# Norm behind each projection: the squares of tiles 0 to 5 summed by VectorE in PSUM, TensorE multiplies the sum and two tiles at the end

## The chip, the core and the metric

One core of a Trainium2 chip runs the whole program. The metric is the device time of one execution in microseconds (us), as the median of several runs.

## What is computed

Two transformer blocks over 256 positions and 1024 channels, one after the other, in float32. Most of the work is large matrix products; between them stand root-mean-square norms over the channels:

```python
def rms_norm(x, g):
    xf = x.astype(jnp.float32)
    y = xf * lax.rsqrt(jnp.mean(xf * xf, axis=-1, keepdims=True) + NORM_EPS)
    return (y * g.astype(jnp.float32)).astype(x.dtype)

# first block
    mix = jnp.concatenate([o_rw, o_nsa, o_s5], axis=-1).astype(h.dtype) @ w_out[i]
    h = h + rms_norm(mix, post_mix_norm[i])                              # norm 1
    f = conv_ffn(rms_norm(h, pre_ffn_norm[i]), w_up[i], conv_w[i], conv_b[i], w_down[i])   # norm 2
    h = h + rms_norm(f, post_ffn_norm[i])                                # norm 3
    e = rms_norm(p[i] @ w_ple[i], ple_norm[i])                           # norm 4
    gate = jax.nn.sigmoid((h @ w_ple_gate[i]).astype(jnp.float32)).astype(h.dtype)
    h = h + gate * e
# second block, for each of two layers
        h = _modulate(_rmsnorm(x, norm1_g[layer]), sh1, sc1)             # norms 5 and 7
        ...
        x = x + g1[:, None, :] * y
        h = _modulate(_rmsnorm(x, norm2_g[layer]), sh2, sc2)             # norms 6 and 8
        x = x + g2[:, None, :] * _conv_ffn(h, ffn_w_up[layer], ...)
    return _rmsnorm(x, final_g)                                          # norm 9
```

## The kernel before

**Tiles.** The residual `h` lies transposed: 8 tiles of 128 channels by 256 positions. A projection has 8 output tiles (`job`s), each in one of the 8 PSUM banks, which are handed out in rotation (`next_bank`, line 477); TensorE waits until the bank's last job has been read by the engine that frees it (`freed`). `close` (535) counts `psum_ready` up by one when a job is done, and readers wait for their job's number.

**Split weights.** Products of a projection are made in three passes (`three_passes`, 558): high part of the weight by high part of the activation, high by low, low by high. A weight chunk is 128 by 2048 floats (two output tiles). SyncE's queue loads it into one of 6 ring slots. ScalarE writes its high part (`hi_ready`), GpSimd subtracts and writes the low part (`low_parts`, 1531, `lo_ready`), strictly in the order in which the chunks are used; there are 4 slots for high parts. `chunk` (509) makes TensorE wait for `lo_ready` of a chunk the first time that it is asked for.

**When ScalarE makes high parts.** It has no fixed place for them. Every time that ScalarE is about to wait for a job (`take` 2327, `gone` 2331), `reach` (2303) first emits all the high parts that are due: those whose chunk four places back in the order (its high slot) and six places back (its ring slot) are used only by jobs before that one. `take0` and plain waits emit none. `root` (2357) and `high_parts` (2361, the high parts of the normalised activations) use these plain waits.

**A norm.** ScalarE squares the tiles (`squares` 2347 for norms 6 to 9, two tiles per instruction for tiles 0 to 5, once VectorE has added the job to `h`; `out_squares` 2567 for norms 1 and 3, from PSUM and together with a copy). TensorE sums over the channels: for every tile two matmuls with the squares as the stationary operand and one column of 1/1024 (`mean_square_of` 603). Then ScalarE takes the root (`root`), VectorE the reciprocal (`norm_scale` 1613), TensorE spreads it over the partitions (`spread` 614), VectorE scales, ScalarE writes the high parts, and TensorE starts the next projection with `first_tiles` (584). This function first opens four tiles and asks for their weights, two chunks, and only then waits for the high part of activation tile 0; it runs the high passes of the four tiles together, k by k, and then the low passes.

**Where the squares are multiplied.** In `last_tile` (634; norms 1, 6, 8) tiles 0 to 5 stand ahead of the last output tile and 6 and 7 behind it. In TensorE's `ffn` (1101; norms 3, 7, 9), whose down projection goes over m = 0 to 3 with two output tiles and three chunks (`("down", f, m, c)`) each, tiles 0 to 3 stand ahead of chunk c = 1 of m = 3, tiles 4 and 5 ahead of c = 2, and 6 and 7 behind.

The chunks behind the down projection of ffn 0 are `("pleg", 0 to 3)`, read by the jobs `pg`; behind that of ffn 1 stand `("kv", 0)`, `("kv", 4)`, `("kv", 8)`, `("kv", 12)`, read by `dk` and `dv`. After norm 3 ScalarE comes to its next `reach` at `take(("pg", 0))` (2635), after norm 7 at `reach(("dk", 0, 0, 0))` (2676).

Of the kernel before, what the change touches and what calls it, by code (L numbers as in the profile page):

```python
# [73 lines left out]
def two_block_kernel(nc, a, out):  # L74
    ctx = ExitStack()
    with ctx:
# [306 lines left out]
        NORM_ORDER = (0, 1, 2, 4, 3, 5, 6, 7, 8, 9)  # L383

        def rs_of(i):
            return rs[:, 4:8] if i == 4 else rs[:, 0:4]
# [69 lines left out]
        def _(pe):  # L456
# [34 lines left out]
            def held_back():  # L491
# [3 lines left out]
                return bank  # L495

            begun = set()

# [84 lines left out]

            def first_tiles(rnd, jobs, x, ks=tuple(range(KT))):

                low, high = x
                todo = []
                for job, key, c0 in jobs:
                    b = opened(job)[:, 0:T]
                    todo.append((b, [v[:, :, c0:c0 + P] for v in chunk(key)]))  # L590
                for n, k in enumerate(ks):
                    pe.wait_ge(sem("x_high"), KT * (rnd + 1) + n + 1)
                    for b, (w_lo, w_hi) in todo:
                        mm(b, w_hi[:, k, :], high[:, k, :], start=(n == 0), stop=False)
                        mm(b, w_lo[:, k, :], high[:, k, :], start=False, stop=False)
                for t, (b, (_, w_hi)) in enumerate(todo):
# [4 lines left out]
                    close(last)  # L601

            def mean_square_of(i, b, sq, ks):

                for k in ks:
                    if k % 2 == 0 or k == KT - 1:
                        pe.wait_ge(sem("squares"), 5 * (i - (i > 4)) + (1, 1, 2, 2, 3, 3, 4, 5)[k])
                    for s in range(2):
                        last = mm(b[:, s:s + 1], sq[:, k, s * P:s * P + P], ones_mean[:, 0:1],
                                  start=(k == s == 0), stop=(k == KT - 1), skip_group_check=True)  # L610
                if ks[-1] == KT - 1:
                    close(last)

            def spread(i, scratch=True):
# [8 lines left out]
            def projection(rnd, name, key, x, ms=None, ks=tuple(range(KT))):  # L623

                tiles = [((name, m), (key, m // 2), 128 * (m % 2)) for m in range(8)]
                first_tiles(rnd, tiles[:4], x, ks)
# [474 lines left out]
            def ffn(f, first, ms):  # L1101
# [5 lines left out]
                for m in range(4):  # L1107
# [14 lines left out]
                    for c in range(3):  # L1122
                        if m == 3 and c:
                            mean_square_of(ms[0], b_ms, ms[1], (0, 1, 2, 3) if c == 1 else (4, 5))
                        key = ("down", f, m, c)
                        w = chunk(key)
                        n = chunk_src[key][0].shape[1]
                        for i in range(2):
                            for k in range(n):
                                t = 8 * c + k  # L1130
                                if m == 0 and i == 0:
                                    pe.wait_ge(sem("act_split"), FT * f + t + 1)
                                last = three_passes(outs[i][:, 0:T], [v[:, k, i * P:i * P + P] for v in w],
                                                    (act_lo[:, t, :], act_hi[:, t, :]), t == 0, t == FT - 1)
                            if c == 2:
                                close(last)
                        if c < 2:
# [192 lines left out]
            pe.wait_ge(sem("x_high"), KT * 10)  # L1330
            pe.wait_ge(sem("x_split"), KT * 10)
            for m, bank in enumerate(out_banks):
                numbered(("dw", m), bank)
                held.remove(bank)
                close(out_passes(m, bank, (6, 7)))
            split_tile(("dw", 6), ("do", 3), 0, (hn_lo, hn_hi))
# [210 lines left out]
        def _(dve):  # L1547
# [62 lines left out]
            def own_done(n):  # L1610
                dve.wait_ge(sem("dve_own"), n)

            def norm_scale(i):
# [468 lines left out]
            def ffn(f):  # L2082
# [47 lines left out]
                if f:  # L2130
                    for m in range(8):
                        b = take(("down", f, m))
                        stt(h[:, m, :], b[:, 0:T], mc(f - 1, 5, m), h[:, m, :], MUL, ADD, *freed(("down", f, m)))

            def modulated(i, n, rnd, low, high, shift, **k):

                return scaled_parts(i, lambda k: gsc[:, 8 * n + k:8 * n + k + 1], rnd, high, low, sem("x_scaled"), shift, **k)

            add_normed(1, "post_mix", yb)
            scaled_parts(2, lambda k: col("pre_ffn", k), 1, hn_hi, hn_lo, sem("x_scaled"))  # L2140
# [24 lines left out]
            for k in range(KT):  # L2165
                stt(eb[:, k, :], eb[:, k, :], col("ple_norm", k), wide, MUL, MUL, sem("eb_scaled"))
            add_normed_split(3, "post_ffn", yb, 2, hn_hi, hn_lo)
            dve.wait_ge(sem("h_copied"), KT)
# [32 lines left out]
            for m in range(8):  # L2201
                b = take(("po", m))
                stt(h[:, m, :], b[:, 0:T], mc(0, 2, m), h[:, m, :], MUL, ADD, *freed(("po", m)))
            settle()
            modulated(6, 1, 5, hn_lo, hn_hi, 24)
# [63 lines left out]
            for m in range(8):  # L2269
                b = take(("dw", m))  # L2270
                stt(h[:, m, :], b[:, 0:T], mc(1, 2, m), h[:, m, :], MUL, ADD, *freed(("dw", m)))
            settle()
            modulated(8, 4, 9, hn_lo, hn_hi, 72)
# [10 lines left out]
        def _(act_):  # L2284
# [45 lines left out]

            def gone(job):

                reach(job)
                act_.wait_ge(*freed(job))
# [277 lines left out]

            out_squares([("out", m) for m in range(8)], yb)
            root(1)
# [8 lines left out]
            for k in range(0, KT, 2):  # L2623
                af(hn[:, k:k + 2, :], eb[:, k:k + 2, :], ACT.Square, sem("eb_squares"))
            out_squares([("down", 0, m) for m in range(4)], yb)
            root(4)
            out_squares([("down", 0, m) for m in range(4, 8)], yb, 4)
            root(3)
# [38 lines left out]
            for m in (6, 7):  # L2667
                pooled(m)
            squares(hn, lambda k: gone(("po", k)))
# [75 lines left out]
            attention_high((6, 7))  # L2745
            squares(hn2, lambda k: gone(("dw", k)))
            root(8)
            modulate(8, 6, hn_hi, 72)
            ffn(2)
            squares(hn, lambda k: gone(("down", 2, k)))  # L2750
            root(9)
# [31 lines left out]
```

## Time and profile before

| | |
|---|---|
| median of 3 runs | 1455.54 us (1453.73 to 1458.12) |
| the profiled execution | 1459.26 us, its span 1457.3 us |
| mean granted TensorE clock | 0.949 of full |
| TensorE matmul busy | 1362.4 us, 93% |
| GpSimd / ScalarE / VectorE busy | 833.8 / 619.2 / 562.4 us |

The profile comes from one execution. Its timeline gives start and duration of each instruction (equal neighbours are merged, with their count), and in brackets how long the engine sat idle before it and who released it. The chain of work that ended last is followed back from the last instruction.

### The profile page before, as it was taken

What the parts mean: (1) busy time and instruction counts of PE and PEld (TensorE: products, weight loads), DVE (VectorE), ACT (ScalarE), POOL (GpSimd) and SP (SyncE); (2) the same over time, 40 slices, a digit from 0 to 9 for tenths busy, and PEclk for the clock granted to TensorE, in tenths of its full rate; (3) what the DMA queues carried; (4) which work ended last, traced back from release to release, by engine and by line L of the source; (5) the groups of instructions that cost most, each with busy time, mean ns of one, the idle gap of its engine ahead of it and who ended that gap; (6) DMA issues with size and microseconds to landing.
All of it is one profiled execution on the core that took longest, in us unless ns stands there. A gap on an engine that the chain in (4) does not pass through costs nothing.

```text
span 1457.3 us, 26522 instructions
## 1 busy us (share of the span) xinstructions
PE 1362.4 (93%) x11138; PEld 1277.3 (88%) x11138; DVE 562.4 (39%) x1241; ACT 619.2 (42%) x925; POOL 833.8 (57%) x419
## 2 busy tenths in 40 slices
PE   6989798979899999989999999999999987999998
PEld 5987355868899999989999999989999877999997
DVE  4645867651255472322433302132233242333301
ACT  3532153223465554544444434544544343554431
POOL 5872430022388878545688775845655443688771
PEclk9998798996899999989999999999999999899998
DMA  7945898330455555434455554443636683455550
GB/s 219 207 123 188 301 383 312 120 112 4 134 171 185 175 180 179 140 108 149 141 177 193 166 188 146 140 132 91 186 91 216 192 286 102 158 178 192 167 159 30
DMA packets 246323, 244.96 MB, mean 168 GB/s; under 512 B 25652, under 2 KB 215230, under 8 KB 246206
## 3 DMA queue, kind: packets, MB, share of 16 engines
q1 hardware_dynamic: 245715, 243.10, 52.2%
q8 instruction: 89, 1.46, 0.4%
q10 hardware_dynamic: 491, 0.17, 0.1%
q14 instruction: 28, 0.23, 0.1%
HBM read 242.20 MB, written 1.05 MB: 167 GB/s over the span
## 4 chain that ended last, share of the span: by engine, by line
PE 83%; DVE 6%; issue 2%; ACT 2%; DMA 2%; POOL 0%; DVEq 0%; ACTq 0%
PE banks L533 82%; DVE arena L1584 2%; DMA ring<-in_attn_w_o_dram 1%; DVE arena L1591 1%; ACT arena L2291 1%; DMA ring<-in_ffn_w_up_dram 1%; PE banks L543 0%; DVE banks L1591 0%; ACT ring_hi L2291 0%; DVE ring_lo L1584 0%; DVE arena L1772 0%; PE banks L818 0%; DVE arena L1588 0%; DVE hn L1591 0%; PE banks L941 0%
## 5 line engine op out<-in xcount | busy, mean ns | idle before, releaser
L1535 POOL TENSOR_TENSOR ring_lo<-ring,ring_hi 128x2048 fp32r<-128x2048 f32 (+1 forms) x176 | 718.7, 4096 | 510.4 <-ACT ring_hi L2291 510.0
L533 PE MATMUL banks<-hn_hi,ring_lo 128*128 128x256 f32 x1888 | 539.1, 289 | 0.0
L533 PE MATMUL banks<-hn_hi,ring_hi 128*128 128x256 f32 x1696 | 484.4, 290 | 7.6 <-ACT hn_hi L2291 7.6
L533 PE MATMUL banks<-hn_lo,ring_hi 128*128 128x256 f32 x1696 | 445.0, 283 | 0.0
L2291 ACT ACTIVATE ring_hi<-ring 128x2048 fp32r<-128x2048 f32 (+1 forms) x176 | 299.7, 1704 | 179.7 <-PE banks L533 131.0
L533 PEld LDWEIGHTS banks<-hn_hi,ring_lo 128*128 128x128 f32 x1888 | 375.2, 199 | 0.0
L533 PEld LDWEIGHTS banks<-hn_hi,ring_hi 128*128 128x128 f32 x1696 | 335.0, 198 | 9.6 <-issue 9.4
L533 PEld LDWEIGHTS banks<-hn_lo,ring_hi 128*128 128x128 f32 x1696 | 310.9, 193 | 0.1
L2291 ACT ACTIVATE arena<-banks 128x256 f32<-128x256 f32 (+5 forms) x229 | 90.3, 411 | 319.1 <-PE banks L533 265.4
L533 PEld LDWEIGHTS banks<-arena 64*128 64x128 f32 (+4 forms) x1282 | 122.7, 188 | 72.4 <-issue 52.3
L533 PE MATMUL banks<-arena 128*64 128x128 f32 (+9 forms) x1282 | 150.4, 314 | 32.1 <-issue 13.2
L533 PE MATMUL banks<-act_hi,ring_hi 128*128 128x256 f32 x528 | 150.1, 284 | 0.0
L533 PE MATMUL banks<-act_hi,ring_lo 128*128 128x256 f32 x528 | 149.4, 283 | 0.0
L533 PE MATMUL banks<-act_lo,ring_hi 128*128 128x256 f32 x528 | 149.4, 283 | 0.0
L1591 DVE SCALAR_TENSOR_TENSOR arena<-banks,par,arena 128x255 f32<-128x255 f32 (+1 forms) x187 | 89.1, 480 | 151.6 <-ACT arena L2291 149.9
L2291 ACT ACTIVATE arena<-banks,par 128x256 f32<-128x256 f32 x88 | 49.8, 565 | 121.5 <-PE banks L533 121.4
L533 PEld LDWEIGHTS banks<-act_lo,ring_hi 128*128 128x128 f32 x528 | 101.3, 192 | 0.0
L533 PEld LDWEIGHTS banks<-act_hi,ring_hi 128*128 128x128 f32 x528 | 101.3, 192 | 0.0
L533 PEld LDWEIGHTS banks<-act_hi,ring_lo 128*128 128x128 f32 x528 | 101.3, 192 | 0.0
L1591 DVE SCALAR_TENSOR_TENSOR h<-banks,mod,h 128x256 f32<-128x256 f32 x32 | 15.5, 484 | 163.4 <-PE banks L533 163.4
L533 PE MATMUL banks<-hn_hi,early_hi 128*128 128x256 f32 x192 | 58.6, 305 | 7.6 <-DVE ring_lo L1584 6.4
L533 PE MATMUL banks<-ring_lo,hn_hi 128*128 128x256 f32 (+1 forms) x224 | 63.7, 284 | 0.0
(236 smaller groups left out, 1706.0 us busy)
## 6 DMA issues: line engine op xcount, KB each, us to landing
ring<-in_ada_w_dram SPq DMA_DIRECT2D x48, 1024.0 KB, 8.3
ring<-in_ffn_w_up_dram SPq DMA_DIRECT2D x44, 1024.0 KB, 5.2
ring<-in_w_up_dram SPq DMA_DIRECT2D x22, 1024.0 KB, 5.1
ring<-in_ffn_w_down_dram SPq DMA_DIRECT2D x16, 1024.0 KB, 5.4
ring<-in_w_kv_dram SPq DMA_DIRECT2D x15, 1024.0 KB, 5.4
ring<-in_w_kv_dram SPq DMA_DIRECT2D x18, 512.0 KB, 3.9
ring<-in_attn_w_q_dram SPq DMA_DIRECT2D x18, 512.0 KB, 3.9
ring<-in_w_in_dram SPq DMA_DIRECT2D x8, 1024.0 KB, 12.1
```

The source lines that it names most:

```text
L533: return nc.tensor.matmul(o, l, r, start=start, stop=stop, **k)
L1535: led.emit(g.tensor_tensor(low, raw, high.bitcast(F32), ALU.subtract), sem("lo_ready"))
L1584: led.emit(v.tensor_tensor(o, x, y, op), signal, value)
L1591: led.emit(v.scalar_tensor_tensor(out=o, in0=x, scalar=s, in1=y, op0=op0, op1=op1), signal, value)
L2291: led.emit(nc.scalar.activation(o, x, func, **k), signal, value)
```

## The change

Norms 1, 3, 6, 7, 8 and 9 are `SUMMED`. For these ScalarE writes the square of tile 0 into a PSUM bank of its own, the job `("acc", i)`, which is opened ahead of the projection's first tile and held until the norm's last matmul. VectorE adds the squares of tiles 1 to 4 to it in place and writes the sum with tile 5 to the place of the square 0 in SBUF. TensorE multiplies no squares ahead of the last tile; behind it it multiplies the sum, tile 6 and tile 7. ScalarE's squares are now one instruction for each tile, and for the output tiles 6 and 7 it calls no `reach` (`limit` 0, or `take0` in place of `take`).

```diff
             def first_tiles(...): ...
+                if ms is not None:
+                    gathered(ms)
...
             def mean_square_of(i, b, sq, ks):
                 for k in ks:
-                    if k % 2 == 0 or k == KT - 1:
-                        pe.wait_ge(sem("squares"), 5 * (i - (i > 4)) + (1, 1, 2, 2, 3, 3, 4, 5)[k])
+                    if i in SUMMED and k == 0:
+                        copied(("acc", i))
+                    elif i in SUMMED:
+                        pe.wait_ge(sem("squares"), square_base[i] + k + 1)
+                    elif k % 2 == 0 or k == KT - 1:
+                        pe.wait_ge(sem("squares"), square_base[i] + (1, 1, 2, 2, 3, 3, 4, 5)[k])
...
             def last_tile(job, key, x, ms):
                 b = opened(job)
                 b_ms = opened(("ms", ms[0]))
-                mean_square_of(ms[0], b_ms, ms[1], (0, 1, 2, 3, 4, 5))
                 ...
-                mean_square_of(ms[0], b_ms, ms[1], (6, 7))
+                mean_square_of(ms[0], b_ms, ms[1], (0, 6, 7))
...
             def ffn(f, first, ms):
+                    if m == 0:
+                        gathered(ms[0])
...
-                        if m == 3 and c:
-                            mean_square_of(ms[0], b_ms, ms[1], (0, 1, 2, 3) if c == 1 else (4, 5))
...
-                mean_square_of(ms[0], b_ms, ms[1], (6, 7))
+                mean_square_of(ms[0], b_ms, ms[1], (0, 6, 7))
...
+            def add_square(i, k, sq):                     # VectorE
+                acc = bank_of(("acc", i))[:, 0:T]
+                dve.wait_ge(sem("squares"), square_base[i] + k + 1)
+                if k == 1:
+                    take(("acc", i))
+                else:
+                    own_done(summed_at[i, k - 1])
+                if k < 5:
+                    tt(acc, sq[:, k, :], acc, ADD)
+                    summed_at[i, k] = led.count["dve_own"]
+                else:
+                    tt(sq[:, 0, :], sq[:, k, :], acc, ADD, *freed(("acc", i)))
...
             for m in range(8):                            # VectorE, norm 8; 6, 7 and 9 alike
                 b = take(("dw", m))
                 stt(h[:, m, :], b[:, 0:T], mc(1, 2, m), h[:, m, :], MUL, ADD, *freed(("dw", m)))
+                if 2 <= m <= 6:
+                    add_square(8, m - 1, hn2)
...
-            def gone(job):
-                reach(job)
+            def gone(job, limit=99):
+                reach(job, limit)
                 act_.wait_ge(*freed(job))
...
+            def summed_squares(i, dst_, after):           # ScalarE
+                sqrt_table()
+                for k in range(KT):
+                    after(k)
+                    o = dst_[:, k, :] if k else take0(("acc", i))[:, 0:T]
+                    af(o, h[:, k, :], ACT.Square, sem("squares"))
...
-            def out_squares(jobs, y, k0=0):
+            def out_squares(i, jobs, y, k0=0):
                 sqrt_table()
                 for k, job in enumerate(jobs, k0):
-                    b = take(job)
-                    af(sqb[:, k, :], b[:, 0:T], ACT.Square, sem("squares") if k % 2 or k == 6 else None)
+                    b = take(job) if k < 6 else take0(job)
+                    o = sqb[:, k, :] if k else take0(("acc", i))[:, 0:T]
+                    af(o, b[:, 0:T], ACT.Square, sem("squares"))
                     af(y[:, k, :], b[:, 0:T], ACT.Identity, *freed(job))
...
-            squares(hn, lambda k: gone(("down", 1, k)))
+            summed_squares(7, hn, lambda k: gone(("down", 1, k), 99 if k < 6 else 0))
```

## Rows read from the trace of the kernel before

**Rows 1.** The page's part 4: shares of the chain that ended last, by engine.
```profile
PE 83%; DVE 6%; issue 2%; ACT 2%; DMA 2%; POOL 0%; DVEq 0%; ACTq 0%
```
**Rows 2.** Timeline, TensorE, norms 1 and 7: matmuls of squares (start us, duration us).
```profile
372.87 2.74 PE L533 MATMUL banks<-ones_mean,arena 128*128 128x1 f32 x24
...
885.47 1.84 PE L533 MATMUL banks<-ones_mean,hn 128*128 128x1 f32 x16
...
893.01 0.95 PE L533 MATMUL banks<-ones_mean,hn 128*128 128x1 f32 x8
...
899.40 0.60 PE L533 MATMUL banks<-ones_mean,hn 128*128 128x1 f32 x4 [0.68 <-ACT hn L2291]
```
**Rows 3.** Timeline, ScalarE, around norm 7.
```profile
880.49 0.63 ACT L2291 ACTIVATE hn<-h 128x512 f32<-128x512 f32 x1 [3.41 <-DVE h L1591]
881.02 1.90 ACT L2291 ACTIVATE ring_hi<-ring 128x2048 fp32r<-128x2048 f32 x1
...
893.21 1.92 ACT L2291 ACTIVATE ring_hi<-ring 128x2048 fp32r<-128x2048 f32 x1 [5.63 <-PE banks L533]
896.77 0.42 ACT L2291 ACTIVATE hn<-h 128x256 f32<-128x256 f32 x1 [1.65 <-DVE h L1591]
...
907.33 0.48 ACT L2291 ACTIVATE hn_hi<-banks,mod 128x256 fp32r<-128x256 f32 x1 [0.44 <-DVE banks L1591]
907.71 1.91 ACT L2291 ACTIVATE ring_hi<-ring 128x2048 fp32r<-128x2048 f32 x1
```
**Rows 4.** Timeline, GpSimd, around norm 7.
```profile
883.00 9.28 POOL L1535 TENSOR_TENSOR ring_lo<-ring,ring_hi 128x2048 fp32r<-128x2048 f32 x2 [2.34 <-ACT ring_hi L2291]
...
909.69 4.64 POOL L1535 TENSOR_TENSOR ring_lo<-ring,ring_hi 128x2048 fp32r<-128x2048 f32 x1 [9.89 <-ACT ring_hi L2291]
```
**Rows 5.** Timeline, TensorE: first matmul after norm 7; first of the fifth tile.
```profile
902.61 0.36 PE L533 MATMUL banks<-hn_hi,ring_hi 128*128 128x256 f32 x1 [1.18 <-ACT hn_hi L2291]
...
915.68 0.28 PE L533 MATMUL banks<-hn_hi,ring_hi 128*128 128x256 f32 x1
```
**Rows 6.** Timeline, ScalarE, around norm 3.
```profile
574.58 1.92 ACT L2291 ACTIVATE ring_hi<-ring 128x2048 fp32r<-128x2048 f32 x1
...
587.77 1.92 ACT L2291 ACTIVATE ring_hi<-ring 128x2048 fp32r<-128x2048 f32 x1 [5.63 <-PE banks L533]
...
604.57 1.91 ACT L2291 ACTIVATE ring_hi<-ring 128x2048 fp32r<-128x2048 f32 x1
```
**Rows 7.** Timeline, TensorE: first matmul after norm 3; first of the fifth tile.
```profile
597.16 0.55 PE L533 MATMUL banks<-hn_hi,ring_hi 128*128 128x256 f32 x1 [1.81 <-ACT hn_hi L2291]
...
611.13 0.28 PE L533 MATMUL banks<-hn_hi,ring_hi 128*128 128x256 f32 x1
```
**Rows 8.** Stretch after norm 6: PE, PEld, DVE, ACT, POOL busy; granted clock, DMA, GB/s.
```profile
703.00:708.00 5.00, 4.97 (x23) 5.00 (x24) 4.82 (x12) 2.81 (x7) 0.00 (x0) 0.50 0.05 12
```
**Rows 9.** Timeline, ScalarE and TensorE, around norm 8.
```profile
1236.05 1.91 ACT L2291 ACTIVATE ring_hi<-ring 128x2048 fp32r<-128x2048 f32 x1 [1.64 <-DMA ring<-in_ffn_w_up_dram]
...
1238.54 1.87 PE L533 MATMUL banks<-ones_mean,arena 128*128 128x1 f32 x8 [3.02 <-ACT arena L2291]
1240.26 0.56 PE L533 MATMUL banks<-hn_hi,ring_hi 128*128 128x256 f32 x1
...
1245.01 0.50 PE L533 MATMUL banks<-ones_mean,arena 128*128 128x1 f32 x4
...
1246.84 0.26 ACT L2291 ACTIVATE rs<-banks,drv 128x2 f32<-128x2 f32 x1 [0.69 <-PE banks L533]
```
**Rows 10.** The page's part 5: busy us, mean ns of one; idle before, and its releaser.
```profile
L1591 DVE SCALAR_TENSOR_TENSOR h<-banks,mod,h 128x256 f32<-128x256 f32 x32 | 15.5, 484 | 163.4 <-PE banks L533 163.4
```
**Rows 11.** Timeline, TensorE and GpSimd, after norm 2.
```profile
399.09 0.35 PE L533 MATMUL banks<-hn_hi,ring_hi 128*128 128x256 f32 x1 [1.09 <-ACT hn_hi L2291]
...
405.87 4.63 POOL L1535 TENSOR_TENSOR ring_lo<-ring,ring_hi 128x2048 fp32r<-128x2048 f32 x1 [26.96 <-ACT ring_hi L2291]
...
410.68 0.28 PE L533 MATMUL banks<-hn_hi,ring_hi 128*128 128x256 f32 x1
```

More of the change, by code:

```diff
@@ L383, in two_block_kernel @@
         NORM_ORDER = (0, 1, 2, 4, 3, 5, 6, 7, 8, 9)
+        SUMMED = (1, 3, 6, 7, 8, 9)
+        square_base, square_count = {}, 0
+        for i in NORM_ORDER:
+            square_base[i] = square_count
+            square_count += 8 if i in SUMMED else 0 if i == 4 else 5
         def rs_of(i):
@@ L495, in held_back, with gathered @@
                 return bank
+            def gathered(i):
+                numbered(("acc", i), held_back())
             begun = set()
@@ L582, in split_rows, with first_tiles @@
                 close(last)
-            def first_tiles(rnd, jobs, x, ks=tuple(range(KT))):
+            def first_tiles(rnd, jobs, x, ks=tuple(range(KT)), ms=None):
                 low, high = x
                 todo = []
+                if ms is not None:
+                    gathered(ms)
                 for job, key, c0 in jobs:
@@ L600, in first_tiles @@
                         last = mm(b, w_hi[:, k, :], low[:, k, :], start=False, stop=(n == KT - 1))
-                    close(last)
+                    close(last, 2 if ms is not None and t == 0 else 1)
             def mean_square_of(i, b, sq, ks):
                 for k in ks:
-                    if k % 2 == 0 or k == KT - 1:
-                        pe.wait_ge(sem("squares"), 5 * (i - (i > 4)) + (1, 1, 2, 2, 3, 3, 4, 5)[k])
+                    if i in SUMMED and k == 0:
[4 more added lines that the diff above has]
+                        pe.wait_ge(sem("squares"), square_base[i] + (1, 1, 2, 2, 3, 3, 4, 5)[k])
                     for s in range(2):
@@ L612, in mean_square_of @@
                     close(last)
+                    if i in SUMMED:
+                        held.remove(bank_no["acc", i])
             def spread(i, scratch=True):
@@ L625, in projection @@
                 tiles = [((name, m), (key, m // 2), 128 * (m % 2)) for m in range(8)]
-                first_tiles(rnd, tiles[:4], x, ks)
+                first_tiles(rnd, tiles[:4], x, ks, ms[0] if ms else None)
                 for t in tiles[4:7]:
@@ L1135, in ffn @@
                             if c == 2:
-                                close(last)
+                                close(last, 2 if m == i == 0 else 1)
                         if c < 2:
@@ L1331, in _ @@
             pe.wait_ge(sem("x_split"), KT * 10)
+            gathered(8)
             for m, bank in enumerate(out_banks):
@@ L1334, in _ @@
                 held.remove(bank)
-                close(out_passes(m, bank, (6, 7)))
+                close(out_passes(m, bank, (6, 7)), 1 if m else 2)
             split_tile(("dw", 6), ("do", 3), 0, (hn_lo, hn_hi))
@@ L1611, in own_done @@
                 dve.wait_ge(sem("dve_own"), n)
+            summed_at = {}
+            def add_square(i, k, sq):
[10 more added lines that the diff above has]
+                    tt(sq[:, 0, :], sq[:, k, :], acc, ADD, *freed(("acc", i)))
             def norm_scale(i):
@@ L2133, in ffn @@
                         stt(h[:, m, :], b[:, 0:T], mc(f - 1, 5, m), h[:, m, :], MUL, ADD, *freed(("down", f, m)))
+                        if 2 <= m <= 6:
+                            add_square(7 if f == 1 else 9, m - 1, hn)
             def modulated(i, n, rnd, low, high, shift, **k):
                 return scaled_parts(i, lambda k: gsc[:, 8 * n + k:8 * n + k + 1], rnd, high, low, sem("x_scaled"), shift, **k)
+            for k in range(1, 6):
+                add_square(1, k, sqb)
             add_normed(1, "post_mix", yb)
@@ L2166, in _ @@
                 stt(eb[:, k, :], eb[:, k, :], col("ple_norm", k), wide, MUL, MUL, sem("eb_scaled"))
+            for k in range(1, 6):
+                add_square(3, k, sqb)
             add_normed_split(3, "post_ffn", yb, 2, hn_hi, hn_lo)
@@ L2203, in _ @@
                 stt(h[:, m, :], b[:, 0:T], mc(0, 2, m), h[:, m, :], MUL, ADD, *freed(("po", m)))
+                if 2 <= m <= 6:
+                    add_square(6, m - 1, hn)
             settle()
@@ L2271, in _ @@
                 stt(h[:, m, :], b[:, 0:T], mc(1, 2, m), h[:, m, :], MUL, ADD, *freed(("dw", m)))
+                if 2 <= m <= 6:
+                    add_square(8, m - 1, hn2)
             settle()
@@ L2611, in ffn @@
                         own(1, j + 1)
-            out_squares([("out", m) for m in range(8)], yb)
+            out_squares(1, [("out", m) for m in range(8)], yb)
             root(1)
@@ L2624, in _ @@
                 af(hn[:, k:k + 2, :], eb[:, k:k + 2, :], ACT.Square, sem("eb_squares"))
-            out_squares([("down", 0, m) for m in range(4)], yb)
+            out_squares(3, [("down", 0, m) for m in range(4)], yb)
             root(4)
-            out_squares([("down", 0, m) for m in range(4, 8)], yb, 4)
+            out_squares(3, [("down", 0, m) for m in range(4, 8)], yb, 4)
             root(3)
@@ L2668, in _ @@
                 pooled(m)
-            squares(hn, lambda k: gone(("po", k)))
+            summed_squares(6, hn, lambda k: gone(("po", k), 99 if k < 6 else 0))
             root(6)
@@ L2745, in _ @@
             attention_high((6, 7))
-            squares(hn2, lambda k: gone(("dw", k)))
+            summed_squares(8, hn2, lambda k: gone(("dw", k), 99 if k < 6 else 0))
             root(8)
@@ L2749, in _ @@
             ffn(2)
-            squares(hn, lambda k: gone(("down", 2, k)))
+            summed_squares(9, hn, lambda k: gone(("down", 2, k), 99 if k < 6 else 0))
             root(9)
```

## The prediction

> **What bounds the kernel now.** I read the chain of work that ended last first: 83% of it is TensorE [rows 1]. So a matmul that is taken out of TensorE's stream is worth its full time, and every wait of TensorE costs its full time. Then I read the timeline around each norm, engine by engine. TensorE's rows show what is taken out [rows 2]. ScalarE's show which instructions stand between its squares [rows 3, 6], and this is the part that decides. GpSimd's show how long a low part takes [rows 4], and TensorE's again when the next projection starts and when its first four tiles are done [rows 5, 7, 11].
>
> The profiled execution took 1459.26 us, 3.7 above the median of 1455.54; I make the sum against the profiled one and take the difference to the median.
>
> **What it removes.** Per norm, 12 matmuls ahead of the last tile (two for each of the tiles 0 to 5). Norm 1 shows them as 24 records in 2.74 us, norm 7 as 1.84 + 0.95 = 2.79 us; the last record's drain is in these, so I take 2.7. TensorE stands in full work on either side, so all of it comes off: 6 x 2.7 = 16.2 us.
>
> The Trainium skill (TensorE: Matmul & The Clock Gate, Back-to-back issue gap) would make them cheaper: matmuls of one column follow each other at about 25 ns. By that the 24 records would be worth 0.6 us and all six norms 3.6 us. The rows show 114 ns a record [rows 2], and the measurement decides.
>
> **What it adds on TensorE.** Two matmuls with the sum at the very end, 2.79 / 12 x 2 = 0.46 us. In norms 6, 7 and 9 they lie in the wait for square 7: tile 6's four records (about 0.5 us) are followed by 0.68 us of idleness [rows 2], so they cost nothing; were the wait gone, they would cost 0.46. In norms 1 and 3 ScalarE squares straight from PSUM, VectorE's step of 0.48 us [rows 10] isn't in that wait, and I let them cost 0.3 each: -0.6 us of gain.
>
> **What it adds elsewhere.** ScalarE gets eight short squares for five; a single one took 0.42 us and a double one 0.63 [rows 3], and it has gaps of 1.7 to 5.6 us there. VectorE gets five adds. No add of this kind is in the rows; the nearest step on a tile takes 0.48 us [rows 10], so 2.4 us a norm, spread over a projection of over 20 us: nothing, or 0.5 where an add stands ahead of the last tile's step. The held bank leaves seven for the rotation; only norm 8 comes near it (below). SyncE's queue waits for the use of chunks by TensorE alone and is moved past nothing.
>
> **What it moves: ScalarE's high parts.** This is where I expect the loss. `gone` and `take` for output tiles 6 and 7 emit no high parts any more. Which stood there? In norm 7, between the square of tiles 4 and 5 (880.49) and that of tile 6 (896.77), ScalarE made three high parts, the first at 881.02, the last at 893.21 [rows 3]. By the rule of `reach` these are kv0, kv4 and kv8: their high slots are last used by the jobs 5 and 6, and so they become due at `gone(6)`, not before. Now they are skipped. `root` and `high_parts` don't emit any, so the next occasion is `reach(("dk", 0, 0, 0))`, behind the eighth high part of the activations, which ends at 907.33 + 0.48 = 907.81 in the times of before. There one high part was made (907.71, kv12); now there are four, kv0 first. And `first_tiles` asks for kv0 and kv4 before it multiplies anything.
>
> - kv0 high: 907.71 + 1.91 = 909.62. GpSimd starts at 909.69, as it did with kv12 [rows 4], and takes 4.64: 914.33. kv4's low part follows, 4.64 (9.28 for two): about 919.0.
> - TensorE starts at 919.0 in place of 902.61 [rows 5], 16.4 us later.
> - Its four first tiles took 13.07 us to 915.68. With all inputs there, the 96 matmuls take 11.59 us, as after norm 2 [rows 11], and in addition what the clock costs: 1.5 to 2.4 us, the excess of the blocks after norms 7 and 3 over it [rows 5, 7]. So they end at 919.0 + 13.4 = 932.4, 16.7 us later than before.
>
> Norm 3 is the same with pleg0, pleg1, pleg2: three high parts from 574.58 to 587.77, and the next `reach` at 604.57 [rows 6]. pleg0 high ends at 606.48, its low part at 611.2, pleg1's at 615.85; the start moves from 597.16 to 615.85. The four tiles took 13.97 us, to 611.13 [rows 7]; now they end at 615.85 + 13.4 = 629.25, 18.1 us later. Together 34.8 us. Later chunks don't add: kv8's low part is ready at 923.6, and needed at 932.
>
> Does something later give it back? Only a wait for a DMA could, if the DMA ran on by itself. But each DMA waits for a slot that TensorE frees, so the stream moves with TensorE. I take no return.
>
> **The clock.** After norm 6 the granted clock is 0.50 for 5 us [rows 8], the lower of its two levels, behind a few us in which TensorE had little to do. A longer idle stretch starts at the same level, so I charge the 1.5 to 2.4 us once per start, as before.
>
> **Norms 1, 6, 8: one high part late, but in time.** Here two of the chunks behind were due earlier, and only ug1 is skipped. It takes uu1's place at the `reach` behind the activations. After norm 2 that low part ran from 405.87 to 410.50, and TensorE comes to ug1 at 410.68 [rows 11]: 0.2 us of room, more after norms 6 and 8, where the first four tiles run at the low clock. Bounds 0 to 1 us each; I take 0.
>
> **Norm 8.** Before, TensorE waited ahead of the last tile for squares 4 and 5, because ScalarE stood at a high part whose weights had not landed (1236.05); it went on at 1238.54, and the last tile ran from 1240.26 to 1245.01, at the low clock [rows 9]. The change takes the wait from that place. What is late next? The last tile and the norm take the banks of dw4 and dw5. VectorE frees them behind its adds of squares 2 and 3; ScalarE was done with these squares at 1236.05 - 1.64 = 1234.4, and four steps of at most 0.48 [rows 10] take VectorE to about 1236.3, when TensorE starts the last tile. It ends at 1239.2 (24 x 0.12, the pitch of rows 11) or, if the clock has fallen, at 1241.1 (4.75 us, as before). VectorE's last step is queued behind the add of square 4, the step of dw6 and the add of square 5: ScalarE gives square 4 at about 1238.4, so this is at 1239.8. From the later of the two: 0.48, 0.42 and two matmuls of 0.60: the root starts at 1241.3 to 1242.9 in place of 1246.84, 3.9 to 5.5 us earlier. I take 4.6, with the 2.7 in it.
>
> **Sum.** Gains: norms 1 and 3: 2.4 each, norms 6, 7, 9: 2.7 each, norm 8: 4.6: 17.5 us. Losses: 34.8 us. Net +17.3: 1476.6 against 1459.26, as a median 1455.54 + 17.3 = 1472.8 us, slower by 1.2%.
>
> **Rivals.**
> - *Faster: the weights aren't in the way.* If TensorE could start after norms 3 and 7 without the skipped high parts, only the gains are left: 1455.5 - 17.5 = 1438.0 us. For it: 16.2 us of matmuls go for certain. Against it: the three high parts stand in the trace exactly where the change skips them, and the read of `lo_ready` is ahead of the first matmul. Chance 0.08.
> - *No change: only one of the two starts is late,* or each by half: 34.8 / 2 = 17.4 against 17.5, 1455.4 us. This needs a `reach` that I have overlooked. Chance 0.05.
> - *Slower still: the squeezed order costs more.* The 0.2 us of room after norm 2 goes, norms 6 and 8 get a stall of their own, and norm 8 gains nothing but its 2.7: 3 x 1 + 1.9 + some 2 for cold starts: 1480 us. It decides where GpSimd's low part of ug1 ends behind the fourth tile. Chance 0.12.
> - The forecast, both starts late by 16 to 19 us each: chance 0.75.
>
> **How the numbers follow.** Bounds of the likeliest case: losses 16.2 to 17.5 (norm 7) and 17.5 to 19 (norm 3), gains 15 to 19.5: net +14 to +21.5 (16.2 + 17.5 - 19.5; 17.5 + 19 - 15), and 2 us for the median: 1468 to 1478. With the third rival the range is 1465 to 1480; the two rivals below it hold 0.13. What can be told from no change is 0.3%, 4.4 us. Slower by more: 0.75 + 0.12 = 0.87. Within: 0.05. Faster: 0.08.
>
> **What would show it.** Right: after norms 3 and 7 TensorE idle for some 19 to 21 us, released by GpSimd's low parts; ScalarE with four high parts in a row behind the activations; no high parts between tiles 5 and 7; no squares ahead of the last tile; TensorE's matmul records fewer by 6 x 20 = 120. Wrong: TensorE starting a few us after the root in norms 3 and 7. The sum would then be off by the whole 34.8 us; nothing else in it is larger than 3 us.

## The result and the profile after

The changed kernel takes 1471.97 us (median of 4 runs, 1468.58 to 1474.35) against 1454.63 us (median of 4) for the kernel before in the same session: a ratio of 1.0125, 95% interval 1.0098 to 1.0152. It is slower by 17.3 us. The forecast said +17.3 and 1472.8 us.

The page's part 1 (busy us, share of the span, instructions), first of the kernel before, then of the changed one:

```profile
PE 1362.4 (93%) x11138; PEld 1277.3 (88%) x11138; DVE 562.4 (39%) x1241; ACT 619.2 (42%) x925; POOL 833.8 (57%) x419
PE 1335.0 (91%) x11018; PEld 1250.2 (85%) x11018; DVE 570.0 (39%) x1271; ACT 621.3 (42%) x937; POOL 833.2 (57%) x419
```

TensorE has 120 records fewer than the 11138 of before, so the matmuls are gone, and the kernel is slower all the same. The waits of TensorE, grouped by what ended them (us in total, times, longest), say where the time went. The two longest waits, 20.5 and 17.6 us, are new; the longest of before was 6.8 us.

```profile
PE banks L543 <- ACT hn_hi L2335: 23.4, 6, 17.6
PE banks L543 <- POOL ring_lo L1553: 20.5, 1, 20.5
```

They are the starts behind norms 3 and 7. First norm 3, its timeline on three engines (start us, duration us, engine, line, operation; in brackets the idle time before it and its releaser). ScalarE (root, then four high parts of weights), GpSimd (their low parts), TensorE (first matmul, which [rows 7] shows for before):

```profile
577.64 0.26 ACT L2335 ACTIVATE rs<-banks,drv 128x2 f32<-128x2 f32 x1 [0.58 <-PE banks L543]
...
588.15 7.31 ACT L2335 ACTIVATE ring_hi<-ring 128x2048 fp32r<-128x2048 f32 x4
```
```profile
590.14 18.05 POOL L1553 TENSOR_TENSOR ring_lo<-ring,ring_hi 128x2048 fp32r<-128x2048 f32 x4 [29.26 <-ACT ring_hi L2335]
```
```profile
599.47 0.55 PE L543 MATMUL banks<-hn_hi,ring_hi 128*128 128x256 f32 x1 [20.54 <-POOL ring_lo L1553]
```

The four high parts stand in one row behind the activations' eight, where [rows 6] has one. GpSimd had been idle for 29.26 us and then makes four low parts at 4.5 us each. TensorE starts when the second of them is done (590.14 + 9.0 = 599.2). Behind norm 7 it is the same. Here is ScalarE from the square of tile 5 to the weights' high parts; [rows 3] is its counterpart:

```profile
880.08 0.42 ACT L2335 ACTIVATE hn<-h 128x256 f32<-128x256 f32 x1 [1.74 <-DVE h L1609]
893.75 0.42 ACT L2335 ACTIVATE hn<-h 128x256 f32<-128x256 f32 x1 [13.26 <-DVE h L1609]
...
897.03 0.26 ACT L2335 ACTIVATE rs<-banks,drv 128x2 f32<-128x2 f32 x1 [0.70 <-PE banks L543]
...
904.31 0.47 ACT L2335 ACTIVATE hn_hi<-banks,mod 128x256 fp32r<-128x256 f32 x1 [0.43 <-DVE banks L1609]
904.69 7.30 ACT L2335 ACTIVATE ring_hi<-ring 128x2048 fp32r<-128x2048 f32 x4
```

The reader is to see the idle 13.26 us ahead of the square at 893.75: that is where the three high parts of [rows 3] stood. ScalarE now sits still there and has the work later, where TensorE waits for it. GpSimd and TensorE in the same place:

```profile
906.66 18.10 POOL L1553 TENSOR_TENSOR ring_lo<-ring,ring_hi 128x2048 fp32r<-128x2048 f32 x4 [26.34 <-ACT ring_hi L2335]
```
```profile
916.01 0.55 PE L543 MATMUL banks<-hn_hi,ring_hi 128*128 128x256 f32 x1 [17.60 <-ACT hn_hi L2335]
```

The profile puts this last wait down to ScalarE's `hn_hi`, but that had been written at 904.31 + 0.47. The wait covers several semaphores, and the second low part, done at about 915.7 (906.66 + 2 x 4.5), is what came last.

The start behind the root (first matmul minus root) is the measure for everything below: norm 3 from 3.10 to 21.83 us, norm 7 from 2.57 to 18.98 us.

### The profile page after: what moved, and what is told of

Same layout as the page of the kernel before. It is cut to its first block and busy times, and to the rows that moved or that the text cites. A ratio compares the mean times of both kernels' runs of the same rounds, so it can differ in the third digit from the quotient of the medians.

```text
span 1466.7 us, 26353 instructions
## 1 busy us (share of the span) xinstructions
PE 1335.0 (91%) x11018; PEld 1250.2 (85%) x11018; DVE 570.0 (39%) x1271; ACT 621.3 (42%) x937; POOL 833.2 (57%) x419
```

## Experiments

Three measures are used. The ratio and its interval come from the timed runs. The two starts behind the root come from the trace. So does the time from the root of norm 1 to the root of norm 9 (the start of ScalarE's rows `rs<-banks,drv`); it leaves out the stretch ahead of root 1, which takes 367 to 382 us in the traces (last section). It is no fine measure either: between root 1 and root 7 two_early_5 and norm8_order have the same instructions, and their traces differ by 4.4 us there (509.97 against 514.33). So a difference of a few us in this column says nothing by itself. "Start 3" and "start 7" are the first matmul behind the root of norm 3 and of norm 7; they hardly vary.

```
kernel                          median us  ratio   95% interval    start 3  start 7  root 1 to 9
before                          1454.6     -       -                3.10     2.57    1066.8
changed                         1472.0     1.0125  1.0098-1.0152   21.83    18.98    1088.5
early_37    3 high parts back   1435.4     0.9851  0.9820-0.9883    3.27     2.56    1051.7
early_all   no limit anywhere   1436.6     0.9865  0.9834-0.9896    3.10     2.57    1052.7
early_3     norm 3 alone back   1456.2     1.0013  0.9990-1.0036    3.10    18.99    1069.3
old_late_37 before + limit      1491.4     1.0232  1.0204-1.0260   21.82    19.00    1102.0
one_early   1 high part back    1462.4     1.0055  1.0035-1.0075   17.37    14.52    1077.4
two_early   2 high parts back   1431.6     0.9830  0.9764-0.9897    3.10     2.57    1051.2
at_root     3 behind the root   1457.1     0.9999  0.9976-1.0022   11.51    11.48    1070.5
squares_out matmuls dropped     1437.7     0.9874  0.9825-0.9922    3.10     2.57    1050.5
two_early_5 as two_early        1437.2     0.9882  0.9856-0.9909    3.10     2.56    1050.3
norm8_order ug0, uu0 moved      1436.7     0.9885  0.9858-0.9912    3.21     2.57    1054.8
```

**The theory** was the forecast's: the high parts that tiles 6 and 7 no longer make cost the two starts, and the rest of the change gains 17.5 us. **The rivals**: the time is lost in the other parts (adds, held bank, late multiplication); the loss is partly given back later; the loss is ScalarE's own time and not GpSimd's.

### Putting the high parts back

```diff
-                    b = take(job) if k < 6 else take0(job)
+                    b = take(job) if k < 6 or i == 3 else take0(job)
...
-            summed_squares(7, hn, lambda k: gone(("down", 1, k), 99 if k < 6 else 0))
+            summed_squares(7, hn, lambda k: gone(("down", 1, k)))
```

> The changed kernel, with the weights' high parts of norms 3 and 7 back where they stood (tile 6 of these two stages makes them again); everything else of the change stays, norms 1, 6, 8 and 9 keep the limit. Theory (deferred high parts): both starts are early again, and only the gains are left: 1455 - 17.5 = 1437 us (1433 to 1442), TensorE starting 2.6 us after root 7 and about 3 us after root 3. Rival A (the adds, the held bank or the late multiplication cost the time, and the high parts only lie beside it): it stays at 1465 to 1472. Rival B (part of the loss had come back later in the stream, so that undoing it gives less): 1443 to 1455.

Measured 1435.4 us, 0.9851 of before: two lines turn a kernel slower by 17 us into one faster by 20. From root 1 to root 9 it is 36.8 us shorter than the changed kernel; the two starts alone make 18.56 + 16.42 = 35.0 of this. ScalarE ahead of the root of norm 7 in this kernel:

```profile
862.17 1.90 ACT L2335 ACTIVATE ring_hi<-ring 128x2048 fp32r<-128x2048 f32 x1
867.08 1.92 ACT L2335 ACTIVATE ring_hi<-ring 128x2048 fp32r<-128x2048 f32 x1 [3.02 <-PE banks L543]
872.84 1.91 ACT L2335 ACTIVATE ring_hi<-ring 128x2048 fp32r<-128x2048 f32 x1 [3.84 <-PE banks L543]
875.52 0.42 ACT L2335 ACTIVATE hn<-h 128x256 f32<-128x256 f32 x1 [0.76 <-DVE h L1609]
...
878.80 0.26 ACT L2335 ACTIVATE rs<-banks,drv 128x2 f32<-128x2 f32 x1 [0.70 <-PE banks L543]
```

The three are back in the gap, and none delays a square: that of tile 6 still waits 0.76 us for VectorE. TensorE then starts 2.56 us behind the root:

```profile
881.36 0.55 PE L543 MATMUL banks<-hn_hi,ring_hi 128*128 128x256 f32 x1 [1.18 <-ACT hn_hi L2335]
```

In norm 7 no high part was in the way of the squares; start 3 is 3.27 us behind its root, so norm 3 doesn't suffer either.

### No limit in any norm

The same for norms 1, 6, 8 and 9 (`take(job)` and `gone(...)` without a limit everywhere).

> The changed kernel with no limit anywhere: norms 1 and 6 to 9 too make their high parts at tile 6. Theory: in norms 1, 6 and 8 ug1 was late but in time, so this is within 2 us of the kernel that restores norms 3 and 7 alone, 1437 us. If norms 1, 6 and 8 had a stall of their own from the limit (0.2 us of room), it is up to 3 us faster than that one. If instead the high part ahead of squares 6 and 7 lengthens the norm, it is 1 to 4 us slower.

Measured 1436.6 us, 1.2 above early_37 with overlapping intervals, and 1.0 us more between roots 1 and 9. In these norms the limit neither costs nor saves what the times can tell: ug1 was late but in time. Only in norm 8 does the trace show something: with the third high part back ahead of its squares 6 and 7, root 8 comes 22.7 us behind VectorE's copy ahead of the output projection, where it is 21.9 in early_37.

### One of the two alone

Norm 3's line of the edit above, without norm 7's.

> The changed kernel with the high parts of norm 3 alone back at tile 6; norm 7 stays as changed. Theory: the two losses stand one behind the other and add up: 1472 - 18.1 = 1454 us (1451 to 1457), that is 16.4 us above the kernel with both restored. Rival (the losses overlap, because the later start takes up the DMA delay of the earlier one): the step from here to both restored is under 12 us, or over 21.

Measured 1456.2 us: start 3 is at 3.10 again, start 7 still at 18.99. The time is 20.8 us above early_37 by the medians and 17.6 by root 1 to root 9, of which the start is 16.4. The losses stand one behind the other and add up.

### The loss without the gain

```diff
-                    b = take(job)
+                    b = take0(job) if jobs[0][0] == "down" and k >= 6 else take(job)
...
-            squares(hn, lambda k: gone(("down", 1, k)))
+            squares(hn, lambda k: gone(("down", 1, k), 99 if k < 6 else 0))
```

> The kernel before with one thing alone of the change: in norms 3 and 7 the tiles 6 and 7 make no high parts; squares and their matmuls as before. Theory: the whole loss without any gain, 1455 + 34.8 = 1490 us (1485 to 1494). Rival A: no more than the 17 us of the full change, 1472 us, were the loss of another part. Rival B (some comes back later): 1475 to 1484.

Measured 1491.4 us, 36.1 above the 1455.3 of before in that session; root 1 to root 9 gives +35.2, and the two starts 18.72 + 16.43 = 35.15. Nothing comes back later. That the last two agree to a tenth is partly luck, since stretches away from the two starts differ by up to 2.2 us from those of before, in both directions. The first rival falls with this and early_37 together: the loss is there without adds and bank, and gone with them.

```profile
616.39 0.55 PE L533 MATMUL banks<-hn_hi,ring_hi 128*128 128x256 f32 x1 [20.54 <-POOL ring_lo L1535]
...
940.56 0.55 PE L533 MATMUL banks<-hn_hi,ring_hi 128*128 128x256 f32 x1 [17.61 <-ACT hn_hi L2291]
```

The waits, 20.54 and 17.61 us, are those of the changed kernel (20.54 and 17.60).

### How many high parts

```diff
+                    if i == 3 and k == 6:
+                        reach(job, 1)
                     b = take(job) if k < 6 else take0(job)
...
-            summed_squares(7, hn, lambda k: gone(("down", 1, k), 99 if k < 6 else 0))
+            summed_squares(7, hn, lambda k: gone(("down", 1, k), 99 if k < 6 else 1 if k == 6 else 0))
```

and the same with 2 in place of 1.

> The changed kernel, but tile 6 of norms 3 and 7 makes one high part (pleg0, kv0) in place of the three that the kernel before made there. Theory (the start waits for GpSimd's low parts of the first two chunks, one after the other behind ScalarE's eight activation parts): with one of the two made early the start comes one low part earlier, 4.6 us in each of the two norms: 1472 - 9.3 = 1463 us. Rival A (ScalarE's time for the high parts themselves delays the start): 1.9 us each, 1468. Rival B (only the first chunk matters): as with all three, 1435.

> The same with two high parts at tile 6 (pleg0 and pleg1, kv0 and kv4). Theory: the first four tiles need these two alone, and the third chunk's low part comes before the fifth tile wants it, so this is as fast as with all three: 1435 us (1431 to 1440). Rival (the third is late too, each chunk costs one low part): 1435 + 9.3 = 1445.

One: 1462.4 us, the starts 21.83 - 17.37 = 4.46 and 18.98 - 14.52 = 4.46 us earlier. That is one low part of GpSimd (4.5 us in the rows above), not one high part of ScalarE (1.9). GpSimd and TensorE behind norm 3 with one high part made early:

```profile
598.84 13.60 POOL L1553 TENSOR_TENSOR ring_lo<-ring,ring_hi 128x2048 fp32r<-128x2048 f32 x3 [22.86 <-ACT ring_hi L2335]
```
```profile
603.71 0.55 PE L543 MATMUL banks<-hn_hi,ring_hi 128*128 128x256 f32 x1 [16.08 <-POOL ring_lo L1553]
```

TensorE starts when the first of these three low parts is done (598.84 + 4.5 = 603.4). Two: the starts are at 3.10 and 2.57, as before. So the step is not even: 4.5 us for the first, 14.3 and 12.0 for the second, because with both first chunks ready the start no longer waits for anything behind the eight activation parts. The third chunk costs nearly nothing: at the fifth tile of norm 3 TensorE waits 0.93 us for its low part (0.14 us in the second trace of this kernel).

```profile
596.61 0.36 PE L543 MATMUL banks<-hn_hi,ring_hi 128*128 128x256 f32 x1 [0.93 <-POOL ring_lo L1553]
```

The two runs of two_early (1430.0 and 1433.1) were too few for a narrow interval. Five more runs gave 1437.2 us:

> The changed kernel with two high parts at tile 6 of norms 3 and 7, timed again in more rounds for a narrow interval. By its first trace it takes 1051.2 us from the root of norm 1 to that of norm 9, as with all three high parts (1051.7): 1435 us (1432 to 1438), 0.985 to 0.988 of the kernel before.

The ratio, 0.9882 (0.9856 to 0.9909), agrees with early_37 within the intervals.

### Where behind the root

```diff
             root(3)
+            reach(("pg", 0), 3)
             x = norm_slots(3)
...
             root(7)
+            reach(("dk", 0, 0, 0), 3)
             modulate(7, 4, hn_hi, 96)
```

> The changed kernel with the three deferred high parts of norms 3 and 7 made right behind the root and ahead of the activations' high parts. Theory: two high parts are not needed one after the other, only 1.9 us of ScalarE and two low parts of 4.6 us of GpSimd stand behind the root: the start is 11.5 us behind the root in norm 7 in place of 19.0, so 7.5 us per norm are won back: 1472 - 15 = 1457 us (1454 to 1460). Rival (the cost is that the high parts aren't made between the squares, wherever they are put behind them): it stays at 1466 to 1472. Rival (only their place behind the eight activation parts costs): 1437 to 1443.

Measured 1457.1 us, and the starts at 11.51 and 11.48 us behind the root where the theory said 11.5: one high part (1.9), two low parts (9.1) and about 0.5 for the root and the handing over. The forecast's 15 us were won back as 14.9 by the medians; by the trace it is 18.0, since start 3 gains 10.3 and not 7.5 (ScalarE's way to the end of the activations is 3 us longer behind norm 3, and this I had not put in). GpSimd's row with the start:

```profile
900.50 18.11 POOL L1553 TENSOR_TENSOR ring_lo<-ring,ring_hi 128x2048 fp32r<-128x2048 f32 x4 [18.85 <-ACT ring_hi L2335]
```
```profile
909.84 0.55 PE L543 MATMUL banks<-hn_hi,ring_hi 128*128 128x256 f32 x1 [10.09 <-ACT hn_hi L2335]
```

Both rivals of this run fall: the place behind the root matters, and neither of the two tried is free. What each costs can be added up from the queue. In the changed kernel ScalarE did not take the weights ahead of its turn. SyncE had issued their loads from 869.47 on, which land in 5.3 us (median), ScalarE stood idle for 13.26 us up to 893.75, and it made kv0's high part only at 904.69, where its program has it. The Trainium skill (TensorE: Matmul & The Clock Gate, Architectural detail: the array is 16× 32×32, not 1× 128×128) says that ScalarE's queue is strictly first in, first out. These rows agree.

### What the matmuls are worth alone

```diff
                 for k in ks:
+                    if i in (1, 3, 6, 7, 8, 9) and k < 6:
+                        continue
```

> The kernel before with one part left out: the twelve matmuls with the squares of tiles 0 to 5 of norms 1, 3, 6, 7, 8, 9 are dropped with their waits (the mean square is then of tiles 6 and 7 alone, so the output is not the reference's). No adds, no held bank, no limit. It is what the change could give at most. Theory: 16.2 us of matmuls, 1.9 us from the freed wait in norm 8, and there two matmuls fewer at the low clock than the change has (0.9): 1455.3 - 19.0 = 1436.3 us (1433 to 1440), as the changed kernel with its high parts back (1435.4 and 1436.6). Rival (the adds, single squares and the held bank cost something that lies on the path): this is 3 us or more faster than those two, below 1432.

Measured 1437.7 us, where 1436.3 was expected and the full change with its high parts back gives 1435.4 and 1436.6. From root 1 to root 9: 1050.5 us against 1051.7 and 1052.7, and 1051.2 and 1050.3 in the two traces of two_early. So no cost of the adds, the single squares and the held bank can be told: the medians put squares_out 1 to 2 us above the two, the trace up to 2 us below them. The rival of this run (3 us or more, below 1432) is not borne out; its fastest run took 1436.3. But the intervals of the ratios are about 1% wide, so a cost of a few us isn't excluded. The gain is that of the dropped matmuls and of the wait in norm 8.

### What ends last in norm 8

```diff
-            summed_squares(8, hn2, lambda k: gone(("dw", k), 99 if k < 6 else 0))
+            summed_squares(8, hn2, lambda k: gone(("dw", k), (99, 99, 0, 0, 0, 0, 1, 0)[k]))
             root(8)
+            reach(("ug", 2, 0), 1)
             modulate(8, 6, hn_hi, 72)
```

on top of two_early.

> The same, and in norm 8 ScalarE's two high parts (ug0, uu0), which stand ahead of squares 2 and 4 and wait there for their weights to land (4.4 and 1.9 us), are moved: ug0 ahead of square 6, uu0 behind the root. Theory (in norm 8 these waits for the DMA set when the squares are done): the squares follow the tiles, the six matmuls with them run ahead of a fall of the clock, the root comes some 5 us earlier, 17 us behind the copy ahead of the output projection in place of 21.9; then uu0's low part (1.9 + 4.6 us behind the root) is last, and the next projection starts 1 to 3.5 us earlier: 1432 us against 1435. Rival (GpSimd or the landing of uu0 ends last anyway, or the later low part stalls the first tiles): 0 to 5 us slower than the other kernel of this call.

Measured 1436.7 against 1437.2 us: the same. (From root 1 to root 9 it is 4.5 us more than two_early_5, but 4.4 of these lie ahead of root 7, where the two kernels are equal.) The root came earlier as the theory said, and it bought nothing. From VectorE's copy ahead of the output projection (`arena<-banks 128x128`, at 1205.66 here) to the root it takes 16.2 us in place of 21.8, and the six matmuls took 1.79 us in place of 2.72. But the next projection starts 24.1 us behind that copy in place of 24.9, because now the low part of uu0 is last:

```profile
1218.41 1.91 ACT L2335 ACTIVATE ring_hi<-ring 128x2048 fp32r<-128x2048 f32 x1 [2.99 <-DMA ring<-in_ffn_w_up_dram]
...
1221.87 0.26 ACT L2335 ACTIVATE rs<-banks,drv 128x2 f32<-128x2 f32 x1 [0.69 <-PE banks L543]
1222.03 1.90 ACT L2335 ACTIVATE ring_hi<-ring 128x2048 fp32r<-128x2048 f32 x1
```
```profile
1220.40 8.98 POOL L1553 TENSOR_TENSOR ring_lo<-ring,ring_hi 128x2048 fp32r<-128x2048 f32 x2 [25.28 <-ACT ring_hi L2335]
```
```profile
1229.74 0.55 PE L543 MATMUL banks<-hn_hi,ring_hi 128*128 128x256 f32 x1 [6.36 <-POOL ring_lo L1553]
```

ug0 lands late (ScalarE waits 2.99 us for the DMA even at square 6), and from there it is 1.91 and two low parts to the start. In this order the start behind norm 8 is set by the landing of its weights and by GpSimd, and it is 0.8 us earlier than before the move. How much another order could win was not tried.

**The version that beats both** is the changed kernel with the high parts back: 0.9851 (early_37) and 0.9882 (two_early_5) of before, 17 to 20 us.

## Why the prediction was right

It was right in its sign, its size and its mechanism. That the median moved by 17.3 us, to the tenth what the sum said, is luck: the interval of the ratio reaches from 14 to 22 us, and the traces, with 21.7 us from root 1 to root 9 and the 2.7 that norm 1 gained ahead of it, give 19.0. By its steps:

- **Norm 3's start.** Forecast: first matmul at 615.85 in place of 597.16, 18.7 us later. Measured behind the root: 21.83 - 3.10 = 18.7. The fifth tile starts 35.9 us behind the root in place of 17.1: 18.8 later, where 18.1 stood in the sum. The block ran 14.05 us, as long as before (13.97) and not 13.4.
- **Norm 7's start.** Forecast 16.4, measured 16.4.
- **No return.** old_late_37 shows it: 35.2 us lost by the trace, 35.15 in the two starts, 34.8 forecast.
- **The gains.** Root 3 behind root 4: 33.24 us in every trace of a changed kernel, 35.76 in both with the old matmuls: -2.5 (forecast 2.4). Norm 1, from the end of tile 6 (372.87 in [rows 2], 363.3 in the changed kernel) to the root: 6.8 to 4.1 us, -2.7 (2.4). Norm 6 (root 5 to root 6): -2.6 (2.7). Norm 7 (root 6 to 7): -2.7 (2.7). Norm 9 (root 8 to 9): -2.1 (2.7). All six: 17 us with norm 8, and 17.5 forecast. Root 4 to root 3 hardly varies, but the stretches of norms 6, 7 and 9 differ by 1.0 to 1.5 us between the traces of kernels with the same instructions in them, so these three say about 2 to 3.6 us each and not 2.7 to a tenth.
- **ug1 in norms 1, 6, 8.** No cost, as forecast (early_all); in norm 8 the limit saves 0.8 us up to the root.
- **Square 7 in norms 6, 7, 9.** 0.24 us of idleness is left where [rows 2] has 0.68, so the two matmuls more fitted into it, as forecast.

Two of its sums are slightly off, and nothing hung on them. The later bound of norm 8's root adds up to 1242.6 (1241.1 + 0.48 + 0.42 + 0.60) and not 1242.9, so the gain there to 4.2 to 5.5 us. The upper bound of the likeliest case adds up to 1479 (1455.5 + 21.5 + 2) and not 1478.

In two places what happened is not what was told.

**Norm 8** gained 4.25 us (copy to root 26.19 before, 21.94 after; forecast 4.6), but not as told. I had the last tile wait for a bank behind VectorE's adds. It didn't: TensorE ran without a gap and was done 4.65 us before the sum. ScalarE's squares, VectorE's last adds and TensorE's matmuls in the changed kernel:

```profile
1249.73 0.71 ACT L2335 ACTIVATE arena<-h 128x256 f32<-128x256 f32 x2
1252.07 1.91 ACT L2335 ACTIVATE ring_hi<-ring 128x2048 fp32r<-128x2048 f32 x1 [1.63 <-DMA ring<-in_ffn_w_up_dram]
1253.89 0.71 ACT L2335 ACTIVATE arena<-h 128x256 f32<-128x256 f32 x2
```
```profile
1254.32 0.43 DVE L1602 TENSOR_TENSOR banks<-arena,banks 128x256 f32<-128x256 f32 x1 [2.62 <-ACT arena L2335]
...
1255.05 0.41 DVE L1602 TENSOR_TENSOR arena<-arena,banks 128x256 f32<-128x256 f32 x1
```
```profile
1255.52 2.72 PE L543 MATMUL banks<-ones_mean,arena 128*128 128x1 f32 x12 [4.65 <-DVE arena L1602]
```

What ended last was the chain of ScalarE's second high part (it waits 1.63 us for its weights), squares 4 and 5, and the add of square 5. Then all six matmuls came at once behind the idle time, at a granted clock of 0.50: 2.72 us, 0.45 each, where I had priced the last two alone. So the wait that was saved and the tail that was added were both larger than I said, and that they came to 4.25 against 4.6 is luck.

**The stretch from root 7 to norm 8.** With the late start (16.4) and norm 8's gain (4.25) root 8 should be 12.2 us later behind root 7, and it is 14.45. The other 2.3 us lie in the attention between. From root 7 to the copy ahead of norm 8's projection, with the late start taken off, all nine traces with the adds and a held bank take 322.1 to 323.8 us, and the kernel before 320.6; old_late_37 and squares_out, which have neither, take 320.0 and 321.1. No single wait holds it: between squares_out and early_37 the shift grows in steps of under 1 us. Part of the 2.3 us may be the variation between executions, since the nine traces alone spread over 1.7. It may also come from the numbers of the banks, which a held bank shifts for all later jobs. Neither was tried, and the cause stays open.

**Rivals.** *Faster*, 1438.0 us if the weights were not in the way, fell for the change itself, and its sum is what early_37 (1435.4) measured once they were out of the way. *No change* (one start late) is what early_3 measured, 1456.2 against 1455.4 forecast for it. *Slower still* fell with early_all.

## What to carry to other kernels

A step that is taken out of a queue for being in the way is not gone: look where the queue emits it next, and who waits there. In a queue that runs in order, a gap in which the engine waits for something else anyway is the free place for preparing the next stage, and the two parts that the next stage needs first must be made in it. Made later, they cost the whole chain behind them: here 4.5 us of GpSimd for the first, and for the second 14.3 and 12.0 us, since the start then waits for ScalarE's eight activation parts, one high part and one low part. And a saving in TensorE's stream, though certain, is to be weighed against what the edit around it moves: here the dropped matmuls were worth 17 us, and the limit at tiles 6 and 7 of two norms (`take0` in norm 3, an argument of `gone` in norm 7) cost 35.

## What the runs showed of the hardware

**The way to norm 1 runs at different clocks from one execution to the next.** The instruction stream up to norm 1 is the same in early_37 and early_all but for one high part, yet root 1 starts at 367.49 in one and 377.22 in the other. The windows of both (stretch, its length, busy of PE, PEld, DVE, ACT, POOL, granted clock, DMA share, GB/s), first early_37, then early_all:

```profile
341.00:346.00 5.00, 4.54 (x49) 4.40 (x50) 3.03 (x8) 2.30 (x3) 2.62 (x1) 1.00 0.02 3
346.00:352.00 6.00, 6.00 (x52) 6.00 (x51) 1.83 (x6) 3.14 (x6) 4.56 (x2) 1.00 0.00 0
```
```profile
341.00:346.00 5.00, 5.00 (x16) 4.16 (x15) 0.00 (x0) 2.77 (x7) 0.00 (x0) 0.50 0.00 0
346.00:352.00 6.00, 6.00 (x35) 4.87 (x35) 0.23 (x1) 3.42 (x6) 0.36 (x1) 0.50 0.00 0
```

In the one TensorE has the full clock (2.4 GHz), in the other the lower of its two levels (1.2 GHz), and it gets 35 records done against 52 in 6 us. In both, TensorE had stood idle for most of 4 us before its clock fell (busy for 0.00 us from 320 to 324 in early_37, for 0.42 us from 324 to 328 in early_all) and then been busy for 3.4 us or more of each 4 from 332 on. Yet the full clock is back for good at 340 in one and only behind 352 in the other; why is not shown. Between the same two of ScalarE's instructions (at 313.28 and 351.91 in early_37, at 316.66 and 361.64 in early_all) the one takes 38.6 us and the other 45.0, which is 6.4 of the 9.7 us. The two traces of one kernel, two_early and two_early_5, differ too: root 1 at 369.11 and 374.24. Of the traces of this case, root 1 starts at 367.4 to 369.1 in four and at 374.1 to 381.8 in the others. Profiled spans can't be compared as wholes: the changed kernel's profile is 9.4 us longer than that of before, the medians differ by 17.3, and from root 1 on the traces differ by 21.7.

**A matmul of one column costs nearly as much as one of 256.** Per matmul (two records) it took 0.23 us at full clock [rows 2] and 2.72 / 6 = 0.45 at 0.50 above, twice as much. That is 0.114 us per record, and the 256-column records next to them follow each other at 0.12 us. In the trace each record has a weight load of its own, and the loads come at the same distance (here for norm 1 of the kernel before):

```profile
372.75 2.77 PEld L533 LDWEIGHTS banks<-ones_mean,arena 128*128 128x128 f32 x24
```

That the loads set the distance is likely, but no run here varies them. The Trainium skill (TensorE: Matmul & The Clock Gate, Back-to-back issue gap) gives about 25 ns as the least distance of two small matmuls. That is a floor, and the same section has weight load and matmul together set the distance in a stream of such pairs, so the prediction's 3.6 us took it for more than it says. The times bear out the measured price: squares_out, which only drops the matmuls and their waits, is 16.6 us faster than before.
